# An expert ring with swapped operands, alternating 64x64 products, and sums moved into the mixer

## What is computed

```python
def expert_block(args):          # hier_moe, for each block of tokens of one expert
    xb, e = args
    return (jax.nn.silu(xb @ w_gate[e]) * (xb @ w_up[e])) @ w_down[e]   # 1024 -> 512 -> 1024

def _wkv_step(S, inp):           # the scan, 16 heads, 2 directions
    r_t, w_t, k_t, v_t, a_t, b_t = inp
    sa = jnp.einsum('zbhvk,zbhk->zbhv', S, a_t)
    S = S * w_t[..., None, :] + sa[..., :, None] * b_t[..., None, :] + v_t[..., :, None] * k_t[..., None, :]
    return S, jnp.einsum('zbhvk,zbhk->zbhv', S, r_t)

mod_l = silu_c @ ada_w[i] + ada_b[i]        # shifts, scales and gates of layer i
def rmsnorm(x, g): ... x * rsqrt(mean(x*x) + eps) * g
```

## Time and profile before

| | us |
|---|---|
| Runs | 4904.73, 4901.6, 4897.2 |
| Median | 4901.6 |
| Span of the profiled execution | 4899.6 |
| First model: SwiGLU 1, sums, mixer, SwiGLU 2 | up to 957 |
| Sums 1 and 2 (L979) | 297 to 337, 958 to 997 |
| Gated MLP, norm, routing 0 | 999 to 1586 |
| Experts, layer 0 | 1586 to 2315 |
| Overflow, combination, RWKV projections | 2315 to 2665 |
| Scan, 8 rounds | 2665 to 4012 |
| Projection, norm, routing 1 | 4012 to 4121 |
| Experts, layer 1 | 4121 to 4849 |
| Combination, final norm | 4849 to 4899 |

### The profile page before, as it was taken

One profiled execution on the slowest core, in us unless ns is written; L12 is line 12 of the kernel. 1 busy time (PEld: TensorE's weight loads), 2 busy tenths in 40 slices (PEclk: granted clock), 3 DMA queues, 4 the chain that ended last, 5 costly groups with the idle time before them and its releaser, 6 DMA issues. The chain is left out here.

```text
span 4899.6 us, 68797 instructions
## 1 busy us (share of the span) xinstructions
PE 4236.2 (86%) x28873; PEld 3247.8 (66%) x28873; DVE 1338.8 (27%) x2979; ACT 474.8 (10%) x844; POOL 351.2 (7%) x471
## 2 busy tenths in 40 slices
PE   7996699989993999998497888898898885999996
PEld 6774368875542777776244776786687774777775
DVE  4533635414104000000423333423433322000001
ACT  1002210011001000000101101110110100000001
POOL 0000000000001000000001021112102100000000
PEclk9978569889695899999697555555555556999998
DMA  6732027612112899998110000000000013999995
GB/s 220 232 115 71 1 70 251 203 51 87 35 60 66 256 306 307 307 307 288 52 58 12 1 1 1 2 1 1 2 1 1 1 62 109 300 309 304 311 304 171
DMA packets 547008, 641.48 MB, mean 131 GB/s; under 512 B 26905, under 2 KB 442185, under 8 KB 546425
## 3 DMA queue, kind: packets, MB, share of 16 engines
q1 hardware_dynamic: 507460, 543.65, 34.8%
q10 hardware_dynamic: 31926, 71.73, 4.0%
q0 software_dynamic: 7424, 23.12, 1.7%
HBM read 611.67 MB, written 26.77 MB: 130 GB/s over the span
## 5 line engine op out<-in xcount | busy, mean ns | idle before, releaser
L1560 PEld LDWEIGHTS bank<-ex_xt,weights 128*128 128x128 f32 x8192 | 945.6, 196 | 52.6 <-issue 52.6
L1560 PE MATMUL bank<-ex_xt,weights 128*128 128x64 f32 x8192 | 954.4, 280 | 1.9 <-DVE ex_xt L1612 1.9
L1575 PE MATMUL bank<-weights,ex_hidden 128*64 128x512 f32 x1024 | 457.6, 600 | 4.3 <-DVE ex_hidden L1617 1.4
L394 PE MATMUL bank<-u,weights 128*128 128x272 f32 (+1 forms) x1408 | 318.0, 389 | 16.6 <-DVEq L415 16.6
L1575 PEld LDWEIGHTS bank<-weights,ex_hidden 128*64 128x64 f32 x1024 | 136.0, 138 | 278.3 <-issue 265.2
L394 PEld LDWEIGHTS bank<-u,weights 128*128 128x128 f32 x1408 | 270.3, 192 | 64.3 <-DVEq L415 17.4
L1617 DVE TENSOR_TENSOR ex_hidden<-ex_silu,bank 128x128 f32<-128x128 f32 x128 | 36.8, 288 | 906.8 <-ACT ex_silu L1593 906.8
L2333 PE MATMUL bank<-sc_xt,sc_bt 64*64 64x64 f32 x2560 | 259.4, 314 | 0.0
L2333 PEld LDWEIGHTS bank<-sc_x,sc_n 64*64 64x64 f32 x2560 | 231.9, 220 | 37.4 <-issue 37.4
L2333 PEld LDWEIGHTS bank<-sc_xt,sc_bt 64*64 64x64 f32 x2560 | 245.9, 220 | 0.0
L2333 PE MATMUL bank<-sc_x,sc_n 64*64 64x64 f32 x2560 | 239.4, 314 | 1.0 <-PEq L2253 1.0
(11 more groups left out here) (499 smaller groups left out, 4628.8 us busy)
## 6 DMA issues: line engine op xcount, KB each, us to landing
weights<-in_moe_w_gate_dram SPq DMA_DIRECT2D x128, 1024.0 KB, 5.4
weights<-in_moe_w_up_dram SPq DMA_DIRECT2D x128, 1024.0 KB, 8.0
weights<-in_moe_w_down_dram SPq DMA_DIRECT2D x128, 1024.0 KB, 8.1
ada_w<-in_ada_w_dram ACTq DMA_DIRECT2D x24, 2048.0 KB, 8.7
weights<-in_w_gate_dram SPq DMA_DIRECT2D x22, 1024.0 KB, 5.8
weights<-in_w_up_dram SPq DMA_DIRECT2D x22, 1024.0 KB, 8.2
weights<-in_w_down_dram SPq DMA_DIRECT2D x32, 704.0 KB, 6.7
weights<-in_ga_w_in_dram SPq DMA_DIRECT2D x16, 1024.0 KB, 5.6
```

Of the source, the lines that this page charges most:

```text
L394: last = nc.tensor.matmul(k.bank[b + side * NB][:, 0:N], w[:, f, c * P:(c + 1) * P], rhs[:, f, 0:N], start=(f == 0), stop=(f == DC - 1))
L1560: last = nc.tensor.matmul(k.bank[2 + q][:, o:o + SLOTS], w[:, f * 256 + c * P:f * 256 + (c + 1) * P], xt[:, s, f * SLOTS:(f + 1) * SLOTS], ...
L1575: last = nc.tensor.matmul(k.bank[4 + 2 * s + n][0:SLOTS, :], hid[:, s, f * SLOTS:(f + 1) * SLOTS], w[:, f * 512:(f + 1) * 512], start=(f = ...
```

## The change

1. The experts get a ring of their own, `ExpertRing`: 18 slots of 1 MB (the 6 of the stream and 12 more), that is three experts. They are started in the routing stage and refilled by SP. The loop is unrolled. A gate or up piece is four of eight feature rows per partition and all 512 columns, contiguous in memory (8 KB a partition); the features are permuted to match, by ACT's copy in the routing. A down piece has whole rows (4 KB). The turned tokens are stationary (64 columns) and 256 columns of weight stream; the two column halves go to partitions 0 to 63 and 64 to 127 in turn. Two transposes of 128x128 and a copy bring the hidden values back to partitions. The down products alternate the halves too.
2. `blocks_matmul` alternates the halves of the partitions; every 64x64 transpose in the matrices is a product with the identity.
3. Layer 0's sums move into the norm stages of the mixer (14, 14, 10 and 10 of the 48 columns, behind each stage's own products), and two head norms move ahead of the norms cq and ckv.
4. One table set with Ln and Exp is loaded ahead of both. The zero rows are written under the attention. ACT stores the token rows. The chunks of gate and up (SwiGLU) go last to first.
5. The stream stops ahead of the RWKV weights and resumes behind expert 30 of layer 0.

```diff
+class ExpertRing:
+    PIECES = 6
+    SLOTS = 18
...
+        s = (self.PIECES * e + j) % self.SLOTS
+        if j < 4:
+            w = a["moe_w_gate_2" if j % 2 == 0 else "moe_w_up_2"][l, e]
+            src = w.rearrange("(p k) m -> p (k m)", k=DC)[:, (j // 2) * 2048:(j // 2) * 2048 + 2048]
...
+            w = a["moe_w_down_2"][l, e]
+            src = w.rearrange("(k p) m -> p k m", p=P)[:, (j - 4) * 2:(j - 4) * 2 + 2, :]
...
 def norm_stage / head_norm_stage (and Prepare part 4, scan_output)
+            nc.scalar.preload_act_table_set("natural_log_exp_and_others")
...
+            if mods is not None:
+                mods.sums(10)            # 14 in head_norm_stage
...
 route_stage, SP
+            for e in range(3):
+                for j in range(k.ring.PIECES):
+                    k.ring.start(sp, a, l, e, j)
...
 experts_stage, SP
-            k.stream.feed(sp, seg, spent, lambda j: (1, 1, 2, 2, 3, 4)[j], 4)
+            for e in range(3, NE):
+                for j in range(ring.PIECES):
+                    sp.wait_ge(spent, 4 * (e - 3) + (1, 1, 2, 2, 3, 4)[j])
+                    ring.start(sp, k.a, l, e, j)
...
 experts_stage, PE
+                    for q in range(4):
+                        f = 4 * j + q
+                        for side in range(2):
+                            w = ring.slot(e, 2 * j + side)
+                            for t in range(2):
+                                last = nc.tensor.matmul(half_cols(k.bank[2 + side], t),
                                                         xt[:, s, f * SLOTS:(f + 1) * SLOTS],
+                                                        w[:, q * 512 + t * 256:q * 512 + t * 256 + 256],
                                                         start=(f == 0), stop=(f == DC - 1))
...
 scan_matrices, PE
-                            if h == 0:
-                                last = nc.tensor.transpose(to, src, k.ident[rows, rows])
-                            else:
-                                last = nc.tensor.matmul(to, src, k.ident[rows, rows], start=True, stop=True)
+                            last = nc.tensor.matmul(to, src, k.ident[rows, rows], start=True, stop=True)
...
 def blocks_matmul(nc, ps, lhsT, rhs):
-    for h in HALVES:
-        rows = slice(h, h + RH)
-        for j in range(NCH):
-            t = slice(j * CH, (j + 1) * CH)
+    for j in range(NCH):
+        t = slice(j * CH, (j + 1) * CH)
+        for h in HALVES:
+            rows = slice(h, h + RH)
             last = nc.tensor.matmul(ps[rows, t], lhsT[rows, t], rhs[rows, t], start=True, stop=True)
```

More of the change, by code:

```diff
@@ L339, in _ @@
                                                    op0=ALU.mult, op1=ALU.mult).then_inc(ready, 1)
+            if mods is not None and mods.columns == 6 * DC:
+                mods.spread(dve)
             if parts[0][3] is not None:
@@ L604, in _ @@
                                  start=True, stop=True).then_inc(summed, 1)
+            if mods is not None:
+                mods.sums(14)
         @block.vector
@@ L968, in share, with sums @@
         self.add(dve, r, b * self.ROUND // of, (b + 1) * self.ROUND // of)
-    def finish(self):
+    def sums(self, count):
+        nc = self.k.nc
+        for m in range(self.columns, self.columns + count):
+            for v in range(2):
+                last = nc.tensor.matmul(self.k.bank[7][:, 2 * m + v:2 * m + v + 1],
+                                        self.acc[:, v, m * P:(m + 1) * P], self.k.ones[:, 0:1], start=True, stop=True)
+        self.columns += count
+        last.then_inc(self.summed, 1)
+        self.parts += 1
@@ L996, in ffn @@
-def ffn(k, n, h, u, T, t0, seg, gains, to):
+                self.sums(6 * DC)
+            block.vector(self.spread)
+def ffn(k, n, h, u, T, t0, seg, gains, to, acc):
     nc = k.nc
@@ L1023, in first_model @@
     k.stream = Stream(nc, ctx, order + more)
+    k.stream.hold = seg["rw_wr_2"].first
+    k.ring = ExpertRing(nc, ctx)
+    k.out_rows = [nc.dram_tensor(f"slot_rows_{l}", ((NE + 2 * T // SLOTS - 1) * SLOTS, D), F32).ap()
+                  for l, T in enumerate((TB, SEQ))]
     k.ident, k.ones, k.head_ones, k.causal = (k.sb(n, [P, P]) for n in ("ident", "ones", "head_ones", "causal"))
@@ L1535, in _, with turn @@
-            pairs(pool, gather)
+            for e in range(NE):
+                if e >= 2:
+                    pool.wait_ge(turned, e - 1)
+                pool.indirect_dma_start(xg[:, e % 2, :], None, rows,
+                                        bass.IndirectOffsetOnAxis(ap=slots[0:SLOTS, e:e + 1], axis=0))\
+                    .then_inc(got[e % 2], 16)
         @block.tensor
         def _(pe):
-            pe.sem_inc(turned, 2)
-            def turn(s):
+            def turn(e):
+                pe.wait_ge(got[e % 2], 16 * (e // 2) + 16)
+                if e >= 2:
+                    pe.wait_ge(copied, e - 1)
@@ L1571, in expert @@
-                for n in range(2):
-                    k.stream.wait(pe, seg, e, 4 + n)
-                    w = k.stream.slot(seg, 4 + n)
-                    for f in range(4):
-                        last = nc.tensor.matmul(k.bank[4 + 2 * s + n][0:SLOTS, :], hid[:, s, f * SLOTS:(f + 1) * SLOTS],
-                                                w[:, f * 512:(f + 1) * 512], start=(f == 0), stop=(f == 3))
+                if e + 1 < NE:
+                    turn(e + 1)
+                pe.wait_ge(gated, e + 1)
@@ new lines, in _ @@
+                for c in range(2):
+                    last = nc.tensor.transpose(k.bank[4][:, c * P:(c + 1) * P], hid[:, s, c * P:(c + 1) * P],
+                                               k.ident[:, :])
+                last.then_inc(hturned, 1)
+                pe.wait_ge(hcopied, e + 1)
+                if e >= 2:
+                    pe.wait_ge(kept, e - 1)
+                for j in range(2):
+                    ring.wait(pe, e, 4 + j)
+                    w = ring.slot(e, 4 + j)
+                    for q in range(2):
+                        o = q * P + j * RH
+                        for n in range(2):
+                            last = nc.tensor.matmul(k.bank[6 + s][n * RH:(n + 1) * RH, :], ht[:, s, o:o + SLOTS],
+                                                    w[:, q * D + n * 512:q * D + n * 512 + 512],
+                                                    start=(j == 0 and q == 0), stop=(j == 1 and q == 1))
@@ L1626, in _ @@
-            copy(0, 0, 0)
-            pairs(dve, expert)
+            for e in range(NE):
+                s = e % 2
+                dve.wait_ge(silued, e + 1)
+                nc.vector.tensor_tensor(hid[:, s, :], act_out[:, s, :], k.bank[3][:, 0:256], ALU.mult)\
+                    .then_inc(gated, 1)
+                dve.wait_ge(hturned, e + 1)
+                nc.vector.tensor_copy(ht[:, s, :], k.bank[4][:, 0:256]).then_inc(hcopied, 1)
+                dve.wait_ge(spent, 4 * e + 4)
+                if e >= 2:
+                    dve.wait_ge(put[s], 32 * (e // 2))
+                nc.vector.tensor_copy(y[:, s, :], k.bank[6 + s][:, :]).then_inc(kept, 1)
@@ L1635, in overflow_stage @@
         sb = lambda n, s, dt=F32: ctx.enter_context(nc.sbuf_tensor(f"ov{l}_{n}", s, dt))
-        w = [sb(f"w{n}", [P, 2048]) for n in range(6)]
+        w = k.ring.slots[RING:RING + 6]
         idx = sb("idx", [SLOTS, 1], I32)
@@ L1835, in moe @@
         norm_stage(k, f"moe_norm{l}", k.x, DC, D, EPS, parts, hm)
+        more = ExitStack()
+        k.ring.place(k, more)
         route_stage(k, l, hm, T, rows, slot_token, table, dest, desti, wts, out_rows)
@@ L1840, in moe @@
     overflow_stage(k, l, nov, rows, slots, tab, out_rows)
+    more.close()
     combine_stage(k, l, T, desti, wts, out_rows)
@@ L1947, in rwkv @@
         lw, la = sb("lw", [P, TB]), sb("la", [P, TB])
-        k.stream.hold = seg["wo"].first
         r, kx, v = (sb(n, [P, DC, TB]) for n in ("r", "k", "v"))
```

270 lines of the change are left out of this document (126 added, 144 removed).

## The result

| | before | after |
|---|---|---|
| Runs, median of 4 (us) | 4903.14 | 3965.87 |
| Lowest and highest | 4897.2 to 4904.73 | 3963.22 to 3967.77 |
| Ratio | | 0.8088, 95% interval 0.8077 to 0.8100 |
| Span of the profiled execution | 4899.6 | 3965.7 |

The account below looks back on a forecast made before the run. TensorE was taken to bound the kernel, at two clock speeds, with DMA close behind in the experts. Terms summed to -971 us from the profiled span of 4899.6, giving 3931 us; 8-in-10 range 3855 to 4190.

Parts of the forecast that it names:

- The experts: Both layers' expert stages: 516 us a layer instead of 726, -420 us for both.
- The DMA bound: In the experts, weight transfers become the limit once PE is faster: 17.4 us an expert.
- Rival (a): Expert weights transfer at the slow end, 351 GB/s: +133 us, 4064 us in all; chance 0.12.
- Rival (c): PE's clock falls for part of the experts: +190 us, 4120 us; only a chance shared with other rivals, 0.10.
- (d): In the experts, products in different columns run one after another: 4421 us in all; chance 0.09.
- (e): In the experts, products neither overlap nor hide their loads: 34.5 us an expert, 5138 us in all; chance 0.02.
- The inversion: Scan inversion with alternating halves: 48 us a round instead of 92.3, the last 30 instead of 76; together -355 us.
- rival (b): The inversion's clock stays at 0.50: +16 us a round, +125 us, 4056 us in all; chance 0.12.
- The matrices: Scan's matrices stage: transposes as products get faster, POOL is late next; -136 us for 8 rounds.
- The sums: Layer 0's sums move into four norm stages and mostly hide there: +11 against 41 saved, -30 us.
- tables: One table set with Ln and Exp saves second loads of 1.28 us in norms and scan outputs: -23 us.
- The routing: Eighteen expert pieces load beside the routing's small transfers, which can be late: +5 us (0 to +30).

Follow-up runs that it names:

- number 6: Changed kernel loading only half of each expert weight piece from expert 3 on (output not the reference's): 3726.7 us in one run.
- number 4: Changed kernel with half-loaded expert pieces and column halves or quadrants alternating after groups of 1, 2, 4 or 8 products: 3924.9 us in one run.
- number 10: Changed kernel with the next round's preparation placed behind the first pair of blocks of each inversion level: 3936.7 us, ratio 0.8024.
- number 2: Changed kernel with the 64x64 transposes of the first half as before, not products with the identity: 4103.2 us, ratio 0.8365.
- numbers 8 and 9: Changed kernel with layer 0's sums in their own stage again: 3990.1 us; changed kernel without the common table set's loads: 3984.8 us.
- number 7: Changed kernel with an expert ring of 12 slots, two experts loaded ahead: 3977.9 us, ratio 0.8114.

## Why the prediction was right, and where it was off

**The experts, -420 forecast, -417.7 measured.** The mechanism holds. PE's need: 7.1 + 3.5 + 2.0 = 12.6 forecast for a full overlap, 12.5 measured in number 6. The overlap of column halves, the bound with no row of its own, came out at 2 rather than 1.6. The DMA bound: 17.4 an expert forecast, 17.2 measured, with the engines full. That the number fits so well is in part luck. The weights needed 6.29/394 = 16.0 us of all engines, not the 15.3 of the sum, since 418 GB/s did not hold; against that, the shares of the queues add up to 1.02 of the window, and the gather took 5.0% of it, 0.9 us an expert, not 1.1. Rival (a) needed a rate of 351 for all weights; the 8 and 4 KB packets had 394. Against the Trainium skill's 358 GB/s in "DMA: Bandwidth & Descriptors", Where 436 GB/s comes from, this single core moved 396 over 380 us; the measurement decides. Rival (c), the clock, showed in part: 0.92 in the steady stretch, and experts with a clock of 0.81 to 0.83 follow at the same 17 us as those with 1.00, so no cost is seen. Rivals (d) and (e) fell: number 4 shows the overlap, and the earlier trace rows hold for the loads.

**The inversion, -355 forecast, -328.5 measured.** This is the term that was off, in size. The 92.3 us a round run from the first instruction of the stage to the end of its last block; measured so, the changed kernel has 51.2, not 48. From first block to first state, as in the table, it is 89.2 to 49.0. Either way a round gains 40 to 41 us, not 44.3, which is most of the 27 us; the last round gained 47.5 where 46 were forecast. The 48 came from the blocks' own chain at one or the other clock. What that chain leaves out is PE's order: 7.7 us of waits for the preparation stand in the list ahead of blocks that could run, and putting blocks first wins 4.1 of them (number 10), more than the 3.2 by which the 48 was too low. The clock did rise, to 0.81 in the mean; the rival (b) of 0.50 throughout is out.

**The matrices, -136 forecast, -140.7 measured,** with POOL last, as forecast; number 2 gives 147 in the matrices for the transposes alone, 137 in the whole kernel.

**The sums, -30; tables, -23; states, -12.** Together -65 forecast; -37.6 up to the first expert and -15.5 in states and output were measured, 12 less. Singly the sums are worth 24 and the tables 19 (numbers 8 and 9), each a little under its term: the products at the ends of the norm stages cost 13.4 us where 11 were taken. Of the states' and outputs' 15.5 the outputs have 8, with their tables, and the states 7.

**The routing, +5 forecast, +9.0 measured,** all in layer 1, where 33 us of routing are too short for 18 MB. It is the price of the stock (number 7).

The terms are off by +2 (experts), +27 (inversion), -5 (matrices), +12 (sums, tables, states), +4 (routing) and -3 (the rest): 37 of 971 us.

## What to carry to other kernels

When a tuned engine is relieved, ask which resource lay close behind it: here the DMA engines at 0.94 told the new bound, and the rates of their queues its time to 1%. In the experts a faster PE is now worth little, since 24 of 32 in a layer follow at the pace of the transfers. When a forecast follows one chain through a stage, look for what else stands in the engine's list between its links: that was the largest miss here. Products in different quadrants or column halves overlap if they stand near each other in the list, so the order of a loop nest is a matter of a factor of up to two; 64x64 transposes alternating with them undo it. And before moving a bulk load earlier, look for the small loads that will share the engines or its queue with it, and for the engine whose issues will hold up the end of a stage.

## What was not expected of the hardware

- The overlap looks about four records ahead: groups of two products cost nothing (7.1 us), of four 1.2 us, of eight 4.5 us, where all in a row would be 14.2 by estimate.
- 2368 tiny packets, 0.17 MB, took 32 us beside large packets of another queue, and 3.4 us alone.
- A job of eight 64x64 transposes alternating with eight products took 5.12 us at clock 0.50, a block of sixteen products half after half 2.7.
- SP was held up to 13.8 us in one issue while its own queue was full of 1 MB pieces.
- One core moved 396 GB/s over 380 us with weights in packets of 4 and 8 KB, and 381 with 2 and 4 KB.
